# Seven half-size products in place of eight for 17 weight slabs of a hybrid encoder layer, with GpSimd making the sums of weights and activations

## What is computed

```python
h = rmsnorm(x, g1)
proj = h @ w_in                       # xa, ya, uv, z, xbc, dt and the three gates
y_a = rglru_branch(...) @ w_a_proj    # gated linear recurrence
y_b = sgu_branch(...)   @ w_b_proj    # spatial gating
y_c = ssd_branch(...)   @ w_c_proj    # chunked scan, then a norm over groups
merged = sig(g_a) * y_a + sig(g_b) * y_b + sig(g_c) * y_c
x = x + merged @ w_out
q = rmsnorm(x, g2) @ w_q ;  k, v = split(rmsnorm(mem, g3) @ w_kv)
x = x + softmax(q k^T / 16) v @ w_o   # 4 heads over 256 memory tokens
x = x + moe(rmsnorm(x, g4))           # 32 experts, 2 per token, 1024 -> 2*512 -> 1024
out = rmsnorm(x, g5)
```

## Time and profile before

| what | value |
|---|---|
| median of three runs (lowest, highest) | 1020.7 us (1019.31, 1021.73) |
| the profiled execution's own time | 1017.95 us |
| its span, first to last instruction | 1016.1 us |
| PE busy, PEld busy | 868.5 us (85%), 634.0 us (62%) |
| DVE, ACT, POOL busy | 244.5, 192.1, 17.8 us |
| DMA | 285.12 MB, mean 281 GB/s |

### The profile page before, as it was taken

How to read it: one execution, slowest core, us unless ns; L and a number is a source line. 1 busy time by engine, 2 the same in 40 slices (tenths; PEclk the granted TensorE clock), 3 DMA queues, 4 the chain that set the end, 5 groups by cost and what they waited for, 6 DMA issues and landing times.

```text
span 1016.1 us, 15322 instructions
## 1 busy us (share of the span) xinstructions
PE 868.5 (85%) x6808; PEld 634.0 (62%) x6808; DVE 244.5 (24%) x654; ACT 192.1 (19%) x347; POOL 17.8 (2%) x25
## 2 busy tenths in 40 slices
PE   9999999999999999999999999666766666666574
PEld 8888856888888888888658655333333333333332
DVE  2353001734041211020210534212211211221222
ACT  2322146741012000010220212111011111101112
POOL 1000000002000000010001000000000000000000
PEclk9999999999999999999999999979888997988988
DMA  8733533524344468444455599999999999999994
GB/s 297 240 138 131 189 130 139 181 90 156 129 171 166 166 268 335 142 166 165 166 208 206 221 426 426 428 426 427 427 428 426 428 426 428 426 426 426 428 425 198
DMA packets 62391, 285.12 MB, mean 281 GB/s; under 512 B 6692, under 2 KB 11640, under 8 KB 50168
## 3 DMA queue, kind: packets, MB, share of 16 engines
q1 hardware_dynamic: 52736, 278.96, 68.8%
q10 hardware_dynamic: 9592, 5.19, 1.9%
HBM read 283.08 MB, written 1.06 MB: 280 GB/s over the span
## 4 chain that ended last, share of the span: by engine, by line
PE 65%; DMA 23%; SPq 5%; another core or an unknown queue 2%; DVE 2%; issue 1%; ACT 1%; DVEq 0%
PE bank L1225 42%; DMA ring<-in_w_gate_up_dram 10%; DMA blk<-in_w_down_dram 8%; PE bank L1237 5%; PE bank L1533 5%; DMA blk<-in_w_gate_up_dram 5%; SPq L375 4%; PE bank L1553 3%; SPq L407 2%; PE bank L1298 1%; PE bank L1517 1%; PE bank L1509 1%; PE bank L1421 1%; PE bank L1441 1%
## 5 line engine op out<-in xcount | busy, mean ns | idle before, releaser
L1225 PE MATMUL bank<-blk,ring 128*128 128x256 f32 x1984 | 432.4, 380 | 2.4 <-DVE blk L947 1.5
L1225 PEld LDWEIGHTS bank<-blk,ring 128*128 128x128 f32 x1984 | 375.8, 190 | 55.3 <-DVE blk L947 1.9
L1533 PE MATMUL bank<-ring,cbm 128*32 128x256 f32 x1088 | 78.9, 438 | 45.1 <-DMA ring<-in_w_gate_up_dram 44.8
L1533 PEld LDWEIGHTS bank<-ring,cbm 128*32 128x32 f32 x1088 | 39.1, 123 | 79.7 <-issue 55.6
L1533 PE MATMUL bank<-blk,cbm 128*32 128x256 f32 x768 | 53.8, 427 | 30.8 <-DMA blk<-in_w_gate_up_dram 30.8
L1097 DVE TENSOR_TENSOR cbm<-bank,gq 128x256 f32<-128x256 f32 x33 | 14.0, 424 | 259.1 <-PE bank L1517 259.1
L1533 PEld LDWEIGHTS bank<-blk,cbm 128*32 128x32 f32 x768 | 28.0, 119 | 51.3 <-issue 32.2
L1553 PE MATMUL bank<-ring,cbm 128*32 128x256 f32 x576 | 38.3, 408 | 24.9 <-DMA ring<-in_w_down_dram 23.8
L1237 PE MATMUL bank<-ring,blk 128*128 128x512 f32 x128 | 55.8, 592 | 0.0
L706 ACT ACTIVATE cbm<-bank 128x128 f32<-128x128 f32 x32 | 8.9, 277 | 242.4 <-PE bank L1533 242.4
L560 ACT ACTIVATE blk<-bank 128x512 f32<-128x512 f32 x28 | 16.7, 597 | 168.7 <-PE bank L1225 168.6
(11 more groups left out here) (274 smaller groups left out, 615.0 us busy)
## 6 DMA issues: line engine op xcount, KB each, us to landing
ring<-in_w_gate_up_dram SPq DMA_DIRECT2D x34, 2048.0 KB, 49.8
blk<-in_w_gate_up_dram SPq DMA_DIRECT2D x24, 2048.0 KB, 50.2
ring<-in_w_in_dram SPq DMA_DIRECT2D x19, 2048.0 KB, 7.7
ring<-in_w_down_dram SPq DMA_DIRECT2D x18, 2048.0 KB, 50.3
blk<-in_w_down_dram SPq DMA_DIRECT2D x10, 2048.0 KB, 50.3
params<-in_w_gate_up_dram SPq DMA_DIRECT2D x6, 2048.0 KB, 50.0
ring<-in_w_kv_dram SPq DMA_DIRECT2D x4, 2048.0 KB, 8.2
params<-in_w_down_dram SPq DMA_DIRECT2D x3, 2048.0 KB, 51.3
```

The costliest lines, as they stand in the source:

```text
L1225: last = mm(ps[:, f * T:(f + 1) * T], w[:, k, c:c + P], src[:, k, :], start=k == 0, stop=k == KD - 1)
L1533: last = mm(gu_bank(p)[c * WIN:(c + 1) * WIN, 0:2 * SEG], xe[:, xin, 4 * j + k, :], w[:, k, :, c, :], start=4 * j + k == 0, stop=4 * j + k ...
```

## The change

**Seven products.** 17 slabs (all of the gates, projections, w_out, k and q but the first slab, gA's first half) are computed by Strassen's method in Winograd's form. A slab's weights are cut into quarters w11, w12, w21, w22 (512 rows of input by 256 outputs), the activations into x11, x12, x21, x22 (512 features by 128 tokens). A product is 8 matmuls with 128 tokens moving; there are seven where plain blocks have eight.

**The two norms** now write their reciprocals into the banks of `cn0`, `cn1` and `xn0`:

```diff
-            dve.wait_ge(read["cn"], 2)
-            link(v.reciprocal(crms, crms))
+            merge("A", 1)
+            fold("gB", 0, gateT, 0)
+            dve.wait_ge(sem["c_rms"], 2)
+            for i in range(2):
+                link(v.reciprocal(halves(bank(f"cn{i}")), crms[:, 2 * i:2 * i + 2, :]))
             for f in range(KD):
                 last = v.scalar_tensor_tensor(out=ycT[:, f, :], in0=ycT[:, f, :], scalar=col("gssm", f),
...
+                if f % 4 == 3:
+                    last.then_inc(read["cn"], 1)
```

**SP** issues the experts' first four parts after the last of the 17 slabs:

```diff
-            sp.wait_ge(sem["unit_done"], U["pC0"] + 1)
+            sp.wait_ge(read["s"], 4 * len(SEVEN))
             for k in range(4):
                 part(k // PARTS, k % PARTS, TURNS[k])
```

```diff
-            scatter(NE - 1, 1)
             pe.wait_ge(sem["ov_ready"], 1)
             n_ov = pe.value_load(ov_i[0:1, 0:1], min_val=0, max_val=NOV)
+            scatter(NE - 1, 1)
```

More of the change, by code:

```diff
@@ L78, in encoder_kernel, with seven @@
     order += [f"sg{i}" for i in range(4)] + ["y7"]
+    SEVEN = {}
+    def seven(name, h):
+        j = SEVEN[name, h] = len(SEVEN)
+        return [f"s{4 * j + r}" for r in range(4)]
     for b in "ABC":
-        for h in (0, 2):
-            order += [f"g{b}{h}", f"g{b}{h + 1}", f"p{b}{h}", f"p{b}{h + 1}"]
+        for h in range(2):
+            order += [f"g{b}0", f"g{b}1"] if (b, h) == ("A", 0) else seven("g" + b, h)
+            order += seven("p" + b, h)
         if b == "A":
@@ L386, in _ @@
                     sp.dma_start(prow[row:row + n, tile, :], ap).then_inc(sem["par1_loaded"], 16)
-            early = SLAB_OF["wo1"]
-            for n in range(1, early):
+            for n in range(1, NSLAB - 1):
                 slab(n)
-            sp.wait_ge(sem["unit_done"], U["pC0"] + 1)
+            sp.wait_ge(read["s"], 4 * len(SEVEN))
             for k in range(4):
                 part(k // PARTS, k % PARTS, TURNS[k])
[L393 to L398, removed]
+            for k, last in ((4, "sc3"), (-1, ""), (5, "va3"), (6, "pt3"), (7, "o3"), (8, "ao1"), (9, "ao3"), (10, "tr3")):
+                if k < 0:
+                    slab(NSLAB - 1)
+                    continue
                 sp.wait_ge(sem["unit_done"], U[last] + 1)
@@ new lines, in in_two, with fold @@
+            def in_two(ps):
+                return ps.rearrange("p (f t) -> p f t", f=2)
+            def fold(name, h, out, f0):
+                j = SEVEN[name, h]
+                sums(j, quarter_of(out, f0, 1, 1)).then_inc(read["s"], 1)
+                dve.wait_ge(sem["product"], 6 * j + 6)
+                v.tensor_tensor(quarter_of(out, f0, 0, 0), mid_a, in_two(part_of(j, 2, 0)), ALU.add)
+                v.tensor_tensor(quarter_of(out, f0, 0, 1), mid_p, in_two(part_of(j, 2, 1)), ALU.add).then_inc(read["s"], 1)
+                take(f"s{4 * j + 3}")
+                v.tensor_tensor(quarter_of(out, f0, 1, 0), mid_q, in_two(part_of(j, 3, 0)), ALU.add).then_inc(read["s"], 1)
@@ L958, in _ @@
[L958 to L959 removed]
+                                              in1=crms_bank(f * GROUPS // KD), op0=ALU.mult, op1=ALU.mult)
+                if f % 4 == 3:
+                    last.then_inc(read["cn"], 1)
+            merge("B", 0)
+            fold("gB", 1, gateT, 4)
             dve.wait_ge(sem["mem_rms"], 1)
@@ L1392, in _ @@
+            for i in range(2):
+                dense(f"gA{i}", hT)
+            pe.wait_ge(sem["yA_ready"], 1)
+            strassen("pA", 0, xaT, TB, 0)
+            strassen("gA", 1, hT, TA, 1)
+            strassen("pA", 1, xaT, TB, 0)
             pe.wait_ge(sem["csum_ready"], 1)
@@ L1536, in ffn @@
                     if j == 0:
-                        if behind:
+                        if behind and not rows:
                             gather(n + 1, 1 - p)
-                        pe.wait_ge(sem["placed_ready"], n + 1 + (xin != p))
+                        pe.wait_ge(sem["placed_ready"], n + 1)
+                        if rows:
+                            pe.wait_ge(sem["gfin_ready"], 1)
                         pe.wait_ge(sem["scat_ready"], n + 1)
```

455 lines of the change are left out of this document (328 added, 127 removed).

## The result

The changed kernel took 1010.7 us (median of four runs, 1010.3 to 1014.7), the kernel before on the same chip 1020.0: ratio 0.991, 95 % interval 0.9894 to 0.9927. Run again later it took 1009.3 us (ratio 0.9888, 0.9874 to 0.9902). The forecast was 1014.8 us, 5.9 less than before: the sign is right, the gain was put 3 to 6 us too low (9.3 and 11.7 were measured).

What follows compares the result with a forecast made beforehand. TensorE was taken to bound the kernel to about 577 us, then DMA of expert weights. Terms -16.5 + 10.7 + 2.0 + 1.0 - 2.1 - 1.0 = -5.9 us took 1020.7 to 1014.8 us, range 1007 to 1023.

Steps and rivals of the forecast that it cites:

- What bounds it, and the gain passes to the end: Whole kernel: TensorE bounds up to about 577 us, then expert weights by DMA; a gain ahead of 577 moves the second half.
- The first parts: First four parts of the experts' weights, issued after the last slab: no cost, 20 us at most if not hidden.
- Part 1, the products: The 17 slabs: 112 instructions at 0.1147 us, 12.85 us a slab for 13.82, -16.5 us in all.
- rival D: Slab products: 128 columns cost half of 256, 0.109 us, 11 us less, GpSimd gives back 3: 1007 us; chance 0.12.
- Part 2, the wait: Ahead of pB.0: TensorE waits for banks until VectorE has scaled for the group norm, +10.7 us, plus a clock loss.
- The clock: Behind the wait ahead of pB.0: a still TensorE loses its clock, +2.0 us (1.6 to 2.8).
- Part 3, GpSimd: GpSimd's sums in the slabs: under 5 % to spare, small waits of TensorE, +1.0 us (0 to 3).
- Part 4: Ahead of wo.0 and sc0: the waits of 1.45 us and 0.65 us go, -2.1 us.
- Part 5, the end: After the last expert: register read moved ahead of the last scatter, -1.0 us (0 to -1.5); no gain behind x3_done.
- B: Slabs: GpSimd sets the pace; 10 % longer operations give about 1024 us, slower from 8 %; chance 0.12.
- C: Slabs: each product starts with a bare weight load, 119 waits at 0.10 us, +12.1 us, 1026.9 us; chance 0.12.

Runs made afterwards that it cites:

- experiment 1: Changed kernel with VectorE inverting the roots and scaling ycT ahead of the fold of gB.0 instead of behind it: 994.9 us, ratio 0.9749.
- experiment 4: Changed kernel with half of each slab's first GpSimd sum made twice, 1.27 us more a slab: 1020.9 us, ratio 1.001.
- experiment 10: Kernel before with the experts' first four weight parts issued some 115 us later, behind the read of the queries: 1020.6 us, ratio 0.9997.
- experiment 5: Changed kernel whose 17 slabs stream 64 of 128 columns, with the same weights and releases: 1066 us.
- experiment 2: Changed kernel with TensorE's wait ahead of pB.0 filled by 46 matmuls that nobody reads: 1008.0 us, ratio 0.9866.
- 7: Kernel before with only the change's new end (gain spread early, register read ahead of the scatter, squares in halves, scaling split): 1022.9 us, ratio 1.0017.
- 8: Changed kernel with the end of the kernel before put back: 1009.5 us, ratio 0.9893.
- 9: Changed kernel with reciprocals and scaling ahead of gB.0's fold, and the end of the kernel before put back: 994.1 us, ratio 0.9752.
- 3: Changed kernel with the norm's reciprocals kept in SBUF instead of the banks, still behind gB.0's fold: 1005.8 us, ratio 0.9848.
- experiment 6: Changed kernel with reciprocals and scaling ahead of gB.0's fold, and 64 of 128 columns in the 17 slabs: 1014.6 us.

## Why the prediction was right, and where it was off

**What bounds it, and the gain passes to the end: right.** What was won or lost in the slabs showed at the end: 12.5 us in the slabs of experiment 1, 14.4 in all; in experiment 4 10.7 lost there, 11.0 in the spans. One reading was off: TensorE falls to six tenths from slice 25 on, not 23, and nothing rests on it. The first parts cost nothing late (experiment 10), and DMA is full behind the first expert.

**Part 1, the products: the mis-sized term.** The step that failed is "3.67 / 32 = 0.1147 us"; the slabs have 0.1117, so 17 slabs give -22.3 us and not -16.5. The chosen row has a start and an end of its own in only 32 instructions, and 0.10 us off the first was not enough. The same 32 in order of time, in the kernel before:

```profile
229.00 3.84 PE L1378 MATMUL bank<-params,blk 128*128 128x128 f32 x32
```

Without the last one's own 0.275 us and the 0.10 of the first that is 3.465 us for 31 steps, 0.1118, so the row held the true pace. The 0.003 us for each of 1904 instructions is the whole error. Where a per-instruction price is multiplied by 1904, the ends of a row of 32 have to come off first. Its reason held: the load of 128 columns of weights sets the pace, since 64 columns moving have the same (0.1121, experiment 5). The value lies between the chosen one and the low end of 0.109; rival D had a bit over half of its 11 us. The gap rule of the Trainium skill (TensorE: Matmul & The Clock Gate, Back-to-back issue gap) gives 109 ns with each column counted twice, an estimate, some 2 % under the measured pace. The 107 ns that the Trainium skill (same title, LDWEIGHTS (loading the stationary operand)) gives a load of 128 columns are 4 % under.

**Part 2, the wait: right in place, cause and size.** Forecast 10.7, measured 10.5, released by the eighth scaling, and experiment 1 took it away by order alone. The clock: forecast 2.0, measured 2.4 in one profile, 2.0 in the second and 1.8 by experiment 2. The words "before, the same work lay beside gB's matmuls and cost nothing" were the better half of it: put there again, it costs nothing again.

**Part 3, GpSimd: right in size, not in place.** Forecast 1.0, measured 0.6: 0.4 at wo.0's second product, for the first sum of mergedT, which stood under "elsewhere", and 0.2 at pA.1's fourth, where 0.1 us to spare were forecast. At the third sum of q.0, which had 0.6 of the forecast, TensorE did not wait. 2.35 and 1.27 us a sum are the earlier trace rows's, but only some of them wait for the one before: four of 1024 take 9.6 us for the 9.8 forecast, four of 512 5.0 for 5.4. That made up for the slabs' faster pace. The margin is thin at more places than those named: experiment 4 lost 11.6 of 22 us, where its own expectation said 7. The scan of the earlier trace rows takes 1.31 us for 0.68 when a sum of GpSimd lies beside it (1.31 to 1.33 in the profiles with this order of sums, 2.67 in experiment 4, where a later sum lies there). The shared ports of the Trainium skill (SBUF — State Buffer, Who interferes with whom), which the prediction left out of its sum, agree in kind; the 0.6 us here are less than the 0.9 that the prediction took from it.

**Part 4: right.** Both waits are gone.

**Part 5, the end: wrong by its cause.** -1.1 us in the two traces for -1.0 forecast looks like a hit and is luck. For the read of the register is not the pause's cause (experiments 7 and 8), and the new end as a whole is worth nothing (8 and 9). The 1 us is in the trace because the new products' programs have next to none of the pause, with either end.

**Rivals.** B needed 10 % more of GpSimd's time, and its operations took what the earlier trace rows say. By experiment 4 it prices well: 22 us more, a tenth of GpSimd's 211, would have taken the gain. C is out: 119 waits and the pace of 12.51 a slab leave nothing for bare loads. The sum by the measured terms, -22.3 + 10.5 + 2.4 + 0.6 - 2.1, is -10.9; with 1.2 lost at the first expert it is -9.7, and -9.3 and -11.7 were measured. The forecast's -5.9 is short by the pitch, 5.8 us; the 1.0 of the end, which it had and which isn't there, and the 1.2 at the first expert, which it hadn't, hid part of that.

## What to carry to other kernels

A resource that passes round (here the banks) joins two engines' queues: before moving work into it, follow what stands ahead of its release on the other engine. Here VectorE released the banks only behind a sum that waits for the slab just before the one that wanted them, and that took 12.5 us in the slabs, of the 26.1 that the change is worth with the other order of two blocks (14.4 in all, of which some 2 are the clock at the first expert). And a price that will be multiplied by thousands is taken from a long piece without waits, or its start and end are taken off first.

## What the hardware showed that I had not expected

- Eight VectorE products of 256 columns took 3.2 us beside GpSimd with one operand in PSUM, and 18.1 us with all in SBUF: 2.57 us each at the median, one for one with GpSimd's sums, some of which slowed from 2.35 to 2.53 (experiments 1 and 3). With all in SBUF and GpSimd idle they took 3.3 (before).
- After 10.5 us without work TensorE came back to full clock in 6 us in the changed kernel, and with 64 columns moving only after 76 us, though its busy row was full (experiment 5, one profile). Without the hole the same matmuls kept the full clock (experiment 6). At half clock an instruction of this kind took 0.214 us for 0.112, so what sets its pace, the load of the weights, slows with the clock too.
- A pause of 1.4 to 1.8 us of TensorE ahead of its last four matmuls came and went with the rest of the program, at the same instructions.
